# Prompt attention of a decoder layer: POOL scales the exponentials, and the value products give the transposed output

## What is computed

```
q, k, v, u = project_in(rmsnorm(yp, mix_norm[l]), w_in[l])
o_a = merge_by_denominator([dilated_branch_prompt(q, k, v, slopes, wdw, dil)
                            for (wdw, dil) in ((128, 1), (512, 4), (2048, 16))])
# in a branch: s = q.k / sqrt(64) - slope * distance where valid; p = exp(s - max);
#              den = sum(p); num = p @ v;   merged: sum(scale * num) / sum(scale * den)
yp = yp + concatenate([o_a, o_b]) @ w_out[l]
```

## Time and profile before

| | |
|---|---|
| Time, median of 3 runs | 2571.97 us (2570.71 to 2573.04) |
| Profiled execution, its own time | 2569.81 us |
| Its span, first to last instruction | 2568.0 us |
| Instructions | 48261 |
| TensorE busy | 2474.9 us (96%) |
| DVE busy | 1206.5 us (47%) |
| ACT busy | 658.5 us (26%) |
| POOL busy | 1199.5 us (47%) |
| Mean granted TensorE clock | 0.988 of full speed |

### The profile page before, as it was taken

How to read it: one execution, slowest core, us unless ns; L and a number is a source line. 1 busy time by engine, 2 the same in 40 slices (tenths; PEclk the granted TensorE clock), 3 DMA queues, 4 the chain that set the end, 5 groups by cost and what they waited for, 6 DMA issues and landing times.

```text
span 2568.0 us, 48261 instructions
## 1 busy us (share of the span) xinstructions
PE 2474.9 (96%) x17695; PEld 2331.9 (91%) x17695; DVE 1206.5 (47%) x2551; ACT 658.5 (26%) x1671; POOL 1199.5 (47%) x1110
## 2 busy tenths in 40 slices
PE   7999999999999999999999999899899999999998
PEld 7999999999999999766558999679799999999997
DVE  5653333333336799434433433533953333333335
ACT  4321111111113233365222223321321111111113
POOL 7466666666666345022001220213176666666662
PEclk9999999999999999999999999999999999999999
DMA  7211111111112122354864113741011111111112
GB/s 244 90 46 45 46 45 45 47 46 49 49 50 74 42 67 76 115 171 132 348 235 135 50 68 129 290 145 42 17 53 47 45 45 49 45 45 45 45 49 95
DMA packets 216000, 224.78 MB, mean 88 GB/s; under 512 B 12090, under 2 KB 183670, under 8 KB 211795
## 3 DMA queue, kind: packets, MB, share of 16 engines
q1 hardware_dynamic: 199399, 195.46, 23.5%
q10 hardware_dynamic: 16492, 27.82, 3.0%
HBM read 190.84 MB, written 32.40 MB: 87 GB/s over the span
## 4 chain that ended last, share of the span: by engine, by line
PE 91%; DVE 5%; ACT 2%; DMA 1%; issue 1%; ACTq 0%; DVEq 0%; SPq 0%
PE ps L963 26%; PE ps L964 26%; PE ps L965 25%; PE ps L1451 2%; PE ps L1495 1%; PE ps L1465 1%; PE ps L1370 1%; PE ps L1383 1%; PE ps L1561 1%; DMA cK<-in_cache_mem_k 1%; PE ps L1544 1%; DVE ps L2490 1%; PE ps L1353 1%; DVE hl L2467 0%; PE ps L1389 0%
## 5 line engine op out<-in xcount | busy, mean ns | idle before, releaser
L963 PE MATMUL ps<-hh,wh 128*128 128x272 f32 (+2 forms) x2528 | 781.2, 309 | 16.6 <-ACT gated L1691 7.1
L965 PE MATMUL ps<-hl,wh 128*128 128x272 f32 (+2 forms) x2528 | 779.3, 308 | 0.0
L964 PE MATMUL ps<-hh,wl 128*128 128x272 f32 (+2 forms) x2528 | 779.2, 308 | 0.0
L798 POOL TENSOR_TENSOR wl<-raw,wh 128x512 fp32r<-128x512 f32 x384 | 496.1, 1292 | 30.7
L963 PEld LDWEIGHTS ps<-hh,wh 128*128 128x128 f32 x2528 | 478.9, 189 | 23.4 <-ACT gated L1691 7.4
L796 POOL CAST wh<-raw 128x512 fp32r<-128x512 f32 x384 | 235.3, 613 | 530.1 <-PE ps L965 460.8
L964 PEld LDWEIGHTS ps<-hh,wl 128*128 128x128 f32 x2528 | 478.0, 189 | 0.5
L965 PEld LDWEIGHTS ps<-hl,wh 128*128 128x128 f32 x2528 | 477.4, 189 | 0.0
L2354 DVE SCALAR_TENSOR_TENSOR x<-ps,x 128x384 f32<-128x384 f32 (+1 forms) x528 | 279.9, 534 | 196.8 <-PE ps L965 194.7
L788 POOL CAST wh<-raw 128x1024 fp32r<-128x1024 f32 x52 | 55.7, 1072 | 627.1 <-PE ps L965 425.0
L963 PE MATMUL ps<-hidh,wh 128*128 128x384 f32 (+1 forms) x1056 | 345.5, 327 | 0.6 <-DVE x L2354 0.5
(11 more groups left out here) (278 smaller groups left out, 3318.2 us busy)
## 6 DMA issues: line engine op xcount, KB each, us to landing
raw<-in_ffn_gate SPq DMA_DIRECT2D x88, 256.0 KB, 2.9
raw<-in_ffn_up SPq DMA_DIRECT2D x88, 256.0 KB, 2.9
raw<-in_ffn_down SPq DMA_DIRECT2D x88, 256.0 KB, 2.7
Kw<-in_cache_win_k SPq DMA_DIRECT2D x24, 512.0 KB, 5.9
Vw<-in_cache_win_v SPq DMA_DIRECT2D x24, 512.0 KB
raw<-in_w_in SPq DMA_DIRECT2D x20, 512.0 KB, 3.8
Kw<-in_cache_win_k SPq DMA_DIRECT2D x8, 1024.0 KB, 8.6
Vw<-in_cache_win_v SPq DMA_DIRECT2D x8, 1024.0 KB
```

The lines of the kernel that those rows point to most:

```text
L798: pool.tensor_tensor(ring_lo(r), quadrant(q), ring_hi(r).bitcast(F32), ALU.subtract).then_inc(s["lo"], 1)
L963: pe.matmul(out, w_hi_, a_hi, start=first, stop=False, skip_group_check=more)
L964: pe.matmul(out, w_lo_, a_hi, start=False, stop=False, skip_group_check=more)
L965: return pe.matmul(out, w_hi_, a_lo, start=False, stop=last, skip_group_check=more)
```

## The change

POOL multiplies each head's exponentials in `Sb` by the reciprocal of their row's sum, in place, and the turn waits for that (`A["p"]` for `A["e"]`). DVE takes the reciprocals of the two heads one by one (`inverse`). Value products swap their operands: 64 value columns are the weights, the turned rows move, head 0's result lies on partitions 0 to 63 and head 1's on 64 to 127, and so the result is already turned. `turn_output`, `normalise` and `O2` go. ACT does both exps of step n+1 between its evictions of step n. DVE's `output(n-1)` reads the value products' bank. POOL's sorts stand between its scalings: the first pair's in front, the second pair's behind steps 2 to 4, the next `i`'s first pair's behind steps 11 to 13. POOL splits no unit of `w_out` before its last scaling; SP loads the first two units where it did and the next two behind the loop of the sample attention's loads. The core of the diff:

```diff
@@ SP
-        first_loads("w_out")
+        for j in range(2):
+            load_unit(j, UNIT["w_out"] + j + 1, W["w_out"][:, :, j * P:(j + 1) * P])
...
+        for j in range(2, SLOTS):
+            load_unit(j % 2, UNIT["w_out"] + j + 1, W["w_out"][:, :, j * P:(j + 1) * P])
         sp.wait_ge(B["s_full"], NB)
         load_keys(NB - 1, 1)
@@ POOL
+            def scale(i, n, h):
+                w = far(wsteps[n][1]) + near(wsteps[n][1])
+                pool.wait_ge(A["r"], i * (2 * WN) + (2 * n + h + 1))
+                pool.tensor_scalar(Sb[:, n % 2, h, 0:w], Sb[:, n % 2, h, 0:w], stat[:, n % 4, 2, h:h + 1], None,
+                                   ALU.mult).then_inc(A["p"], 1)
+
+            for m in range(3):
+                sort(0, 0, m)
+            for i in range(H // 4):
+                for n in range(WN):
+                    for h in range(2):
+                        scale(i, n, h)
+                    if 2 <= n < 5:
+                        sort(i, 1, n - 2)
+                    if i + 1 < H // 4 and 11 <= n < 14:
+                        sort(i + 1, 0, n - 11)
@@ TensorE
             def turn(n, h):
                 p, t = wsteps[n]
-                pe.wait_ge(A["e"], i * (2 * WN) + (2 * n + h + 1))
+                pe.wait_ge(A["p"], i * (2 * WN) + (2 * n + h + 1))
...
                     for h in range(2):
-                        mm = pe.matmul(ps[:, 6 + n % 2, 64 * h:64 * h + 64], PT[:, n % 2, h, len(cuts) + k, :],
-                                       vtok[:, p, t + 1 - len(whole) + k, 64 * h:64 * h + 64], start=(k == 0 and h == 0),
+                        mm = pe.matmul(ps[64 * h:64 * h + 64, 6 + n % 2, 0:P],
+                                       vtok[:, p, t + 1 - len(whole) + k, 64 * h:64 * h + 64],
+                                       PT[:, n % 2, h, len(cuts) + k, :], start=(k == 0),
...
-                    for h in range(2):
-                        for r in range(DIL):
-                            mm = pe.matmul(ps[FAR * r:FAR * (r + 1), 6 + n % 2, 64 * h:64 * h + 64],
-                                           PT[0:w, n % 2, h, k, FAR * r:FAR * (r + 1)],
-                                           vfar[0:w, p, 2 * r + k, 64 * h:64 * h + 64], start=False,
+                    for r in range(DIL):
+                        for h in range(2):
+                            mm = pe.matmul(ps[64 * h:64 * h + 64, 6 + n % 2, FAR * r:FAR * (r + 1)],
+                                           vfar[0:w, p, 2 * r + k, 64 * h:64 * h + 64],
+                                           PT[0:w, n % 2, h, k, FAR * r:FAR * (r + 1)], start=False,
...
                 turn(n, 0)
-                if n >= 2:
-                    turn_output(n - 2)
                 if n >= 1:
                     values(n - 1)
                 turn(n, 1)
@@ ACT
-                    if n + 1 < WN:
-                        exp(n + 1, h)
+                    if n + 1 < WN and h == 0:
+                        exp(n + 1, 0)
+                        exp(n + 1, 1)
@@ DVE
-                dve.tensor_tensor(O2[:, n % 2], ps[:, 6 + n % 2, 0:P].rearrange("p (h e) -> p h e", e=HD),
-                                  stat[:, n % 4, 2, :].unsqueeze(2).to_broadcast([P, 2, HD]), ALU.mult
-                                  ).then_inc(A["scaled"], 1)
+            def inverse(n, h):
+                dve.wait_ge(A["e"], i * (2 * WN) + (2 * n + h + 1))
+                dve.reciprocal(stat[:, n % 4, 2, h:h + 1], stat[:, n % 4, 1, h:h + 1]).then_inc(A["r"], 1)
...
-                if n >= 2:
-                    output(n - 2)
+                if n + 1 < WN:
+                    for h in range(2):
+                        inverse(n + 1, h)
                 if n >= 1:
-                    normalise(n - 1)
-            output(WN - 2)
-            normalise(WN - 1)
+                    output(n - 1)
             output(WN - 1)
```

More of the change, by code:

```diff
@@ L217, in decoder_layer @@
         ktok = alloc(g, "ktok", [P, QT, P])
-        O2 = alloc(g, "O2", [P, 2, 2, HD])
+        alloc(g, "below_stat", [P, 4 * HD])
         stat = alloc(g, "stat", [P, 4, 3, 2])
@@ L921, in memory_split, with attention, sort @@
                           unit_hi(j), unit_lo(j), unit_done, i * 4 + (j + 1))
-        def sort_classes():
+        def attention():
             A = S["pa"]
-            for i in range(H // 4):
-                for p in range(2):
+            def sort(i, p, m):
+                src, dst = ((qT, qs), (kTp, kc), (vT, vc))[m]
+                if m == 0:
                     pool.wait_ge(A[f"in{p}"], i * 64 + 64)
@@ L932, in sort_classes @@
                                      qT[:, p].rearrange("c (t j r) -> c t r j", r=DIL, j=FAR)).then_inc(A["sorted"], 1)
[L933 to L938, removed]
+                    return
+                if p == 0 and m == 1:
+                    pool.wait_ge(unit_done, SLOTS + COL["w_out"])
+                    pool.sem_inc(met, 1)
+                pool.tensor_copy(dst[:, p].rearrange("c (r s) -> c r s", r=DIL),
+                                 src[:, p].rearrange("c (s r) -> c r s", r=DIL)).then_inc(A["sorted"], 1)
+            def scale(i, n, h):
[13 more added lines that the diff above has]
+                        sort(i + 1, 0, n - 11)
         for name, n in plan:
             if name == "w_out":
-                sort_classes()
+                attention()
             if name.startswith("ffn"):
@@ L1400, in sample_tokens @@
                 mm.then_inc(A["tok_t"], 1)
[L1402 to L1406, removed]
             scores(0)
@@ L1427, in _ @@
                 turn(n, 1)
-            turn_output(WN - 2)
             values(WN - 1)
-            turn_output(WN - 1)
         arrive(pe)
@@ L2710, in output @@
                     dve.wait_ge(A["tokst"], 32)
-                dve.wait_ge(A["o_full"], i * WN + (n + 1))
+                dve.wait_ge(A["v_full"], i * WN + (n + 1))
                 dve.tensor_copy(oT[:, p, t * P:(t + 1) * P].rearrange("c (j r) -> c r j", r=DIL),
-                                ps[:, 6 + n % 2, P:2 * P].rearrange("c (r j) -> c r j", r=DIL)).then_inc(A["o_free"], 1)
+                                ps[:, 6 + n % 2, 0:P].rearrange("c (r j) -> c r j", r=DIL)).then_inc(A["o_free"], 1)
             for h in range(2):
                 mask(0, h)
+            for h in range(2):
+                inverse(0, h)
             for n in range(WN):
```

## The result

| | before | changed |
|---|---|---|
| Time, median of 5 runs | 2571.97 us | 2590.09 us (2587.39 to 2595.87) |
| Ratio to before (95% interval) | | 1.0078 (1.0064 to 1.0091) |
| Profiled execution | 2569.81 us | 2591.1 us |
| Its span | 2568.0 us | 2589.3 us |
| Prompt attention, first scores to the sample attention's first key turn | 126.9 us | 146.1 us |

The account below looks back on a forecast made before the run. TensorE was taken to bound the kernel (91% of the chain that ended last). Terms -4.9 + 0.5 + 0.3 + 2.3 + 0.8 + 1.5 + 0.7 = +1.2 us on 2571.97 gave 2573 us, range 2566 to 2585.

Parts of the forecast that it names:

- I take the cast: POOL's scaling priced as its one-input cast, 0.15 us + 0.90 per 1000 columns: 0.47 us for 352.
- The rest of the loop: Turn, eviction, exp, reciprocal and hops between one head 0 turn and the next: 2.16 us plus POOL's scaling; +0.5 us overall.
- Rival 1: POOL multiplies at the two-input price, 0.94 us for 352 columns, 1.15 for 448: +13 us, 2585; chance 0.26.
- TensorE's parts: Prompt attention: output turn gone, near values cheaper, far values dearer, changes of array shape: -1.22 us a pass, -4.9 for four.
- Sorts: POOL's sorts between scalings: a sort and two scalings take 3.2 us against steps of about 3.0; +0.3 per pair of batches.
- First batch: First sort waits for the second half's bias, landing at 1101.45, and scaling of n = 3 stands behind it: +2.3 us.
- Starts: The start of each i adds reciprocal, hop and scaling of an otherwise waited-for exp: +0.8 us for two (0 to 1.5).
- Border: Splits of w_out run into the sample attention's start; DVE's `halves` waits out POOL's instruction under way: +1.5 us (0 to 3).
- Units 2 and 3: These units of w_out load late in the sample attention and are split there beside DVE: +0.7 us (0 to 2).

Follow-up runs that it names:

- sorts cut: Changed kernel with the nine POOL sorts of pairs 2 to 4 cut to 8 columns, scaling at full width: 2577.61 us, 1.0036 of before.
- one-column run: Changed kernel with POOL's scaling cut to one column of each row, all else kept: 2568.64 us, 0.9996 of before.
- first version with split heads: Changed kernel with head 0 scaled by DVE out of PSUM, head 1 by POOL as a product of two tensors: 2567.45 us, 0.9987 of before.
- constant's run: Changed kernel with POOL multiplying by a constant 1/128 in place of the column's scalar: 2584.07 us, 1.0045 of before.

## Why the prediction was wrong

- **The step that failed**: "I take the cast", for the price of POOL's multiply, s = 0.47 for 352 columns. It measured 1.16 (1.40 for 448), above both bounds (0.94 and 1.15 by the subtraction): the two rows were taken as ends of a range, though neither was of that operation. The rest of the loop was right: 3.42 less 1.33 is 2.09, against 2.16. With the real scaling the loop measured 3.10 us for 320 columns (sorts cut, turns at 1132.72 and 1135.82) and 3.74 for 448 (changed kernel, 1219.36 and 1223.10), where TensorE's own steps are 2.5 to 3.3. The forecast had the turns waiting for POOL once and hardly elsewhere; in 21 of the 32 steps one waits for it. The one-column run shows 21 us hanging on it.
- **Rival 1** was the right mechanism at the wrong size. It charged 1.15 for 448, which took 1.40. Its 8 us for nine sorts fit: the three beside pair 2 cost 3.2 us on top of the price's 2.9. (Its terms add up to 13.7, not 13.) Its 2585 stood as the range's upper end, with nothing above for a dearer form or for the clock.
- **TensorE's parts** (-4.9, or -1.2 a pair): right to 0.05 us from t = 3 to 7, off by up to 0.13 in single other steps; pairs 1 and 3 got shorter by 1.1 and 0.9. The stage shows -6.9 because pairs 2 and 4 got shorter by 2.4: the last step of each `i` was missed. There the product into O2 and the output turn stood in the chain behind the last values (0.30 and 0.31 us, with their hops 0.84); step t = 7 at the end of the first i went from 10.06 to 8.61.
- **Sorts** (+0.3 for two batches): with the one-column scaling a batch costs 0.0 in pair 2 and 0.3 in pair 3, with the real one 3.2 in pair 2. The cheap scaling, as its premise, carried this term.
- **First batch** (+2.3): the turn starts at 1104.70, forecast 1104.2 for a wait "about 2 us once", measured 1.47. The term was right; what the wait did to the clock behind it had no term, nor had any rival: about 5 us.
- **Starts** (+0.4 each): 0.27 with a cheap scaling (8.61 to 8.88); 2.8 in the changed kernel (11.42).
- **Border** (+1.5): 0 in the changed kernel, where `halves` starts 0.14 us ahead of the end of POOL's subtraction and lasts 0.23. In five other runs it is real: `halves` lasts 1.55 to 2.10 us. The term is right in kind and size, and hangs on where in POOL's instruction `halves` falls, which the sum had not fixed; that it was 0 here is chance.
- **Units 2 and 3** (+0.7): the sample attention took 153.3 us against 156.1, so the term is not to be seen. The clock is the likely reason for the shorter time: it was at its lower level for 3.7 us of the stage, before for 12.7.

Open: 4 of the 21.3 us arise behind the sample attention in code that is the same. The clock goes with them: the lower level lasts 34 us there against 27 before. The first version with split heads also has 34 us of it and takes 3.9 us more than before, the one-column run has 24 and takes 1.4 less. Why the clock falls more often there was not followed.

## What to carry over

An operation that the trace of before does not hold has no price from its neighbours: bound it by the dearest form of its engine and something on top, or try it in another form first. Before putting work on POOL beside DVE, or on DVE beside POOL, look at the DVE operations with SBUF on both sides: here the multiply, the sum of two operands and a small copy lasted to the end of POOL's instruction, the reciprocal of one column did not, and an input in PSUM freed the multiply. A loop through four engines costs by its sum, so what matters is whether TensorE's own step is longer than that sum. A new wait of TensorE can cost its clock for far longer than the wait. And a comparison of stretches holds only where their granted clocks agree.

## What was not expected of the hardware

- POOL's fp32 multiply by a scalar, one input: 0.28 us + 2.5 ns a column (0.21 + 2.5 with a constant). The product with a repeated column, two inputs: 0.19 + 1.67. The split's two-input subtraction: 2.17. The form with the scalar is the dearest, though it has one tensor input. "GPSIMD Engine Reference" of the Trainium skill, section "4.1 Engine selection", calls one-input operations roughly line-rate. The cast, at 0.90 ns a column, does not speak against that; this multiply, at 2.5, does, and the measurement decides.
- DVE's multiply from SBUF takes 0.45 us for 448 columns undisturbed, and one of 256 took 2.28 beside POOL; out of PSUM 448 columns take 0.69, and none of the 64 takes more.
- A wait of TensorE of 1.47 us at 1103.2, behind one of 0.50, was followed by a mean clock of 0.57 over 20 us; 16 turns of 0.11 us, added mostly into these waits, went with 1.00. A wait of 1.30 us in the constant's run was followed by 3.4 us at the lower level alone.
